# A two-block network on one core: six adds and subtractions per norm pair shared with GpSimd, RoPE copies issued by ScalarE, and the last top-k rounds moved ahead of the softmax

## The reference

```python
def rmsnorm(x, g):
    y = x32 * lax.rsqrt(jnp.mean(x32 * x32, axis=-1, keepdims=True) + EPS)
    return (y * g.astype(jnp.float32)).astype(x.dtype)

def second_block(x, ...):
    for l in range(DEPTH_2):
        h = rmsnorm(x, attn_norm[l])
        z = h @ w_in[l]            # q, k, v of branches A to D, index heads, gates
        yA = forgetting_attention(...)                       # softmax over 512 keys, causal
        yB = dsa_attention(rope(qB), rope(kB), vB, rope(qI), rope(kI), wI)
             # index scores, lax.top_k(score, 128), softmax over the selected keys
        r  = retention(rope(qC), rope(kC), vC)
        yD = sliding_window_gqa(rope(qD), rope(kD), vD, sinks)
        x = x + merged @ w_out[l]
        h = rmsnorm(x, ffn_norm[l])
        x = x + (silu(a) * b) @ w_down[l]
    return rmsnorm(x, final_norm)
```

## Time and profile before

| | us |
|---|---|
| median of 3 runs | 3597.19 |
| lowest and highest | 3596.74, 3599.80 |
| the profiled execution's own time | 3599.8 |
| its span from first to last instruction | 3598.5 |
| granted TensorE clock, mean | 0.989 |

### The profile page before, as it was taken

The page is one execution under the profiler, slowest core; times in us unless marked ns, Lnnn a source line. Parts: engine busy times, 40 slices in busy tenths (PEclk is TensorE's granted clock), DMA queues, the critical chain, the costliest instruction groups (busy, mean ns, idle before and its releaser), DMA issues.

```text
span 3598.5 us, 44824 instructions
## 1 busy us (share of the span) xinstructions
PE 3455.8 (96%) x17234; PEld 2744.8 (76%) x17234; DVE 1636.0 (45%) x3017; ACT 1437.1 (40%) x2442; POOL 1395.3 (39%) x627
## 2 busy tenths in 40 slices
PE   6999989988999999999999999999999999999998
PEld 4778889776678887877776778887876776778886
DVE  7986464647430014764453243143855453234143
ACT  3223354554532223354443344343354443334342
POOL 3454434321234443434332434444434333334443
PEclk9999999999999999999999999999999999999999
DMA  7664345321122323222222222323323222222322
GB/s 299 201 245 164 110 157 166 103 94 55 51 71 90 103 87 103 88 68 91 77 78 82 92 81 87 103 91 112 96 76 89 76 73 90 82 82 94 100 93 84
DMA packets 118420, 376.41 MB, mean 105 GB/s; under 512 B 15424, under 2 KB 16320, under 8 KB 117952
## 3 DMA queue, kind: packets, MB, share of 16 engines
q1 hardware_dynamic: 115728, 367.88, 31.6%
q10 hardware_dynamic: 2480, 5.68, 0.5%
HBM read 359.86 MB, written 2.10 MB: 101 GB/s over the span
## 4 chain that ended last, share of the span: by engine, by line
PE 80%; DVE 9%; ACT 4%; issue 3%; DMA 1%; POOL 1%; SPq 0%; ACTq 0%; DVEq 0%; POOLq 0%
PE ps L1389 24%; PE ps L1391 23%; PE ps L1390 23%; DVE b L2273 2%; PE ps L1649 2%; PE ps L1668 2%; ACT b L1731 1%; PE ps L1631 1%; POOL b L2636 1%; DVE b L2309 1%; PE ps L1432 1%; PE ps L1627 1%; PE ps L1691 1%; PE ps L1702 1%; DMA b<-in_w 1%
## 5 line engine op out<-in xcount | busy, mean ns | idle before, releaser
L2636 POOL TENSOR_TENSOR b<-b,b 128x1024 fp32r<-128x1024 f32 (+2 forms) x579 | 1325.1, 2289 | 2131.9 <-ACT b L1731 2129.0
L1389 PE MATMUL ps<-b,b 128*128 128x512 f32 (+1 forms) x4720 | 1793.3, 380 | 67.6 <-POOL b L2636 32.6
L1391 PE MATMUL ps<-b,b 128*128 128x512 f32 (+1 forms) x4720 | 1754.0, 372 | 0.0
L1390 PE MATMUL ps<-b,b 128*128 128x512 f32 (+1 forms) x4720 | 1753.8, 372 | 0.0
L1389 PEld LDWEIGHTS ps<-b,b 128*128 128x128 f32 x4720 | 890.6, 189 | 300.3 <-issue 99.3
L1391 PEld LDWEIGHTS ps<-b,b 128*128 128x128 f32 x4720 | 890.5, 189 | 160.8
L1390 PEld LDWEIGHTS ps<-b,b 128*128 128x128 f32 x4720 | 892.0, 189 | 155.3 <-issue 5.0
L1731 ACT ACTIVATE b<-b 128x1024 fp32r<-128x1024 f32 (+2 forms) x622 | 606.6, 977 | 266.5 <-PE ps L1391 235.6
L2185 DVE SCALAR_TENSOR_TENSOR b<-ps,b,b 128x511 f32<-128x511 f32 x88 | 66.0, 750 | 364.1 <-ACT b L1782 364.1
L2273 DVE CUSTOM_DVE_ANT_0 b<-b,b,b 128x1024 bf16<-128x1024 f32 x112 | 219.5, 1960 | 17.3 <-DMA b<-in_ada 5.8
L1792 ACT ACTIVATE b<-b 128x512 fp32r<-128x512 f32 (+1 forms) x110 | 64.9, 590 | 399.2 <-DVE b L2194 296.5
(11 more groups left out here) (235 smaller groups left out, 2406.1 us busy)
## 6 DMA issues: line engine op xcount, KB each, us to landing
b<-in_w SPq DMA_DIRECT2D x458, 512.0 KB, 3.5
b<-in_ada SPq DMA_DIRECT2D x88, 512.0 KB, 5.3
b<-in_w SPq DMA_DIRECT2D x80, 384.0 KB, 3.1
b<-in_w SPq DMA_DIRECT2D x80, 320.0 KB, 2.9
b<-b SPq DMA_DIRECT2D x176, 64.0 KB, 2.0
b<-in_const SPq DMA_DIRECT2D x24, 256.0 KB, 3.9
b<-in_x SPq DMA_DIRECT2D x1, 2048.0 KB, 16.7
out<-b SPq DMA_DIRECT2D x8, 256.0 KB, 2.0
```

The lines of the kernel that those rows point to most:

```text
L1389: pe.matmul(out, a[0], b[0], start=first, stop=False)
L1390: pe.matmul(out, a[0], b[1], start=False, stop=False)
L1391: return pe.matmul(out, a[1], b[0], start=False, stop=last)
L2636: then(pool.tensor_tensor(wlo[j % NS][:, 0:nk * w], raw[j % NR][:, 0:nk * w], whi[j % NS][:, 0:nk * w].bitcast(F32), ALU.subtract), "lop", j)
```

## The change

Three edits.

1. In all four addnorms the addition to the residual of tiles 1, 3 and 5 goes from DVE to POOL (new event `anp`). In prenorms 5 to 8 the low part of tiles 1, 3 and 5 goes from DVE to POOL (`pnp`). Each such POOL instruction waits for POOL's previous one (`behind`) and for its producer. The instructions are the same, 128x512 subtractions and additions (128x256 in addnorm 1). That is 12 additions and 12 subtractions.
2. The four RoPE DMAs of each tile are issued by ACT right behind its copy, after a wait for that copy, instead of by SP.
3. The last 11 steps of `select(3)` stay in the stage before, so that all 60 selection steps are woven there; `heads("A")` runs without them. The two 8-wide result vectors of MAX8 lie in the first columns of `stat`, which branch A writes too, and so the first maxima of A wait for the finished mask `("m8", l, 3)`.

```diff
-PN = {0: dict(norm=0, N=L), 1: dict(norm=1, N=LC), ...
-      5: dict(norm=9, N=L), 6: dict(norm=10, N=L), 7: dict(norm=11, N=L), 8: dict(norm=12, N=L)}
+PN = {0: dict(norm=0, N=L, low=False), 1: dict(norm=1, N=LC, low=False), ...
+      5: dict(norm=9, N=L, low=True),
+      6: dict(norm=10, N=L, low=True), 7: dict(norm=11, N=L, low=True), 8: dict(norm=12, N=L, low=True)}
...
-        B, last = select(1) + select(2) + select(3)[:9], select(3)[9:]
+        B = select(1) + select(2) + select(3)
         S += weave(F, [do("gap")] * 6 + [do("wi", l=l), do("fg1", l=l), do("gap")] + B[:8] + [do("fg2", l=l)] + B[8:], 1.0)
-        rounds = heads("A")
-        for k, step in enumerate(last):
-            rounds[k + 1].append(step)
...
-        S += weave(F, rounds, 0.325) + [do("takey", l=l, o=0, t=t) for t in range(4)]
+        S += weave(F, heads("A"), 0.325) + [do("takey", l=l, o=0, t=t) for t in range(4)]
...
+def low_of(p, i):
+    return "pnp" if PN[p]["low"] and i in (1, 3, 5) else "pnv"
...
+    def an_event(a, i):
+        return ("anp" if i in (1, 3, 5) else "anv", a, i)
...
 (SP)
-            elif k == "evac" and st["t"]["name"] in ROPES:
...
-                at.wait_ge(*n("ra", name, l, i))
-                for o in range(0, 128, 32):
-                    sp.dma_start(ropes[name][o:o + 32, i, :], Q[x % 2][o ^ 32:(o ^ 32) + 32, :]).then_inc(s[f"d_half{x % 2}"], 16)
 (ACT)
                     act.activation(Q[x % 2][:, :], b[:, :], ACT.Copy).then_inc(up("ra", name, l, i), 1)
+                    if name == "qb":
+                        at.wait_ge(*n("sqp", l, 3, 3))
+                    elif name in ("qd", "kc"):
+                        at.wait_ge(*n("s1", "A", l, 31))
+                    elif name == "qc":
+                        at.wait_ge(*n("s1", "B", l, 31))
+                    at.wait_ge(*n("ra", name, l, i))
+                    for o in range(0, 128, 32):
+                        act.dma_start(ropes[name][o:o + 32, i, :], Q[x % 2][o ^ 32:(o ^ 32) + 32, :]).then_inc(s[f"d_half{x % 2}"], 16)
 (DVE)
         def low(p, i):
+            if low_of(p, i) != "pnv":
+                return
...
-                at.wait_ge(*n("anq", a, i))
-                dve.tensor_tensor(dst[:, i, :], dst[:, i, :], q[:, 0:N], ALU.add).then_inc(up("anv", a, i), 1)
+                if i not in (1, 3, 5):
+                    at.wait_ge(*n("anq", a, i))
+                    dve.tensor_tensor(dst[:, i, :], dst[:, i, :], q[:, 0:N], ALU.add).then_inc(up("anv", a, i), 1)
...
-                        at.wait_ge(*n("sc", l, 3, 3))
+                        at.wait_ge(*n("m8", l, 3))
...
-                w, top = 128 * (j + 1), top2[:, x, :]
+                w, top = 128 * (j + 1), stat[:, 0:16, :].rearrange("p a b -> p (a b)")[:, 8 * x:8 * x + 8]
 (POOL)
+        def low(p, i):
+            if low_of(p, i) == "pnp":
+                slots = p_slots(p)
+                behind()
+                at.wait_ge(*n("pnh", p, i))
+                then(pool.tensor_tensor(HL[:, i, :], slots[i % len(slots)][:, :], HH[:, i, :].bitcast(F32), ALU.subtract),
+                     "pnp", p, i)
...
+            elif k == "pn":
+                if st["i"] > 0:
+                    low(st["p"], st["i"] - 1)
+            elif k == "pnlow":
+                low(st["p"], 7)
+            elif k == "an":
+                a, i = st["a"], st["i"]
+                if i in (1, 3, 5):
+                    slots, N, dst = a_slots(a), AN[a]["N"], CX if a == 1 else X
+                    behind()
+                    at.wait_ge(*n("anq", a, i))
+                    then(pool.tensor_tensor(dst[:, i, :], dst[:, i, :], slots[i % len(slots)][:, 0:N], ALU.add),
+                         "anp", a, i)
```

More of the change, by code:

```diff
@@ L189 @@
 NF = 5
-PN = {0: dict(norm=0, N=L), 1: dict(norm=1, N=LC), 2: dict(norm=3, N=L), 3: dict(norm=5, N=LC), 4: dict(norm=7, N=L),
-      5: dict(norm=9, N=L), 6: dict(norm=10, N=L), 7: dict(norm=11, N=L), 8: dict(norm=12, N=L)}
+PN = {0: dict(norm=0, N=L, low=False), 1: dict(norm=1, N=LC, low=False), 2: dict(norm=3, N=L, low=False),
+      3: dict(norm=5, N=LC, low=False), 4: dict(norm=7, N=L, low=False), 5: dict(norm=9, N=L, low=True),
+      6: dict(norm=10, N=L, low=True), 7: dict(norm=11, N=L, low=True), 8: dict(norm=12, N=L, low=True)}
 AN = {0: dict(norm=2, N=L), 1: dict(norm=4, N=LC), 2: dict(norm=6, N=L), 3: dict(norm=8, N=L)}
@@ L631 @@
     "dve_ret": ("c1v", "rd", "yc", "yg"), "dve_yl": ("nfl", "yl"), "dve_mg": ("mgl",), "dve_out": ("o",),
-    "pool_lo": ("lop",), "pool_rope": ("rp",),
+    "pool_lo": ("lop",), "pool_pre": ("pnp",), "pool_add": ("anp",), "pool_rope": ("rp",),
 }
 SEM_OF = {e: s for s, es in SIGNALS.items() for e in es}
+def low_of(p, i):
+    return "pnp" if PN[p]["low"] and i in (1, 3, 5) else "pnv"
 def number(S, stream):
@@ L665, in low @@
     def low(p, i):
-        mark("pnv", p, i)
+        mark(low_of(p, i), p, i)
     for s in S:
@@ L797, in number @@
             mark("anq", s["a"], s["i"])
-            mark("anv", s["a"], s["i"])
+            mark("anp" if s["i"] in (1, 3, 5) else "anv", s["a"], s["i"])
         elif k == "mixin":
@@ L1146, in program @@
     r = Region(RM)
-    stat, wi, top2 = r.get([128, 32, 5]), r.get([128, 4, 4]), r.get([128, 2, 8])
+    stat, wi = r.get([128, 32, 5]), r.get([128, 4, 4])
     PB = [ctx.enter_context(nc.psum_tensor(f"ps{i}", [128, 512], F32)) for i in range(8)]
@@ L1254, in n_ready @@
             return s["d_x" if nid == 0 else "d_cx"], 16
-        return n(*{2: ("y1", 0, i), 3: ("anv", 0, i), 4: ("y1", 1, i), 5: ("anv", 1, i), 6: ("wo", i),
-                   7: ("anv", 2, i), 8: ("y1", 2, i), 9: ("anv", 3, i), 10: ("xw", 0, i), 11: ("into", 3, i),
+        return n(*{2: ("y1", 0, i), 3: an_event(0, i), 4: ("y1", 1, i), 5: an_event(1, i), 6: ("wo", i),
+                   7: an_event(2, i), 8: ("y1", 2, i), 9: an_event(3, i), 10: ("xw", 0, i), 11: ("into", 3, i),
                    12: ("xw", 1, i), 13: ("into", 4, i)}[nid])
@@ L1370, in source @@
             if ver[0] == "pn":
-                at.wait_ge(*n("pnv", ver[1], k))
+                at.wait_ge(*n(low_of(ver[1], k), ver[1], k))
                 return (HC, LW) if ver[1] in (1, 3) else (HH, HL)
@@ L2305, in dve_program @@
                 if i >= len(slots):
-                    at.wait_ge(*n("pnv", p, i - len(slots)))
+                    at.wait_ge(*n(low_of(p, i - len(slots)), p, i - len(slots)))
                 elif p in (2, 3, 4, 5):
-                    at.wait_ge(*n("anv", p - 2, 7))
+                    at.wait_ge(*n("anp", p - 2, 5))
                 dve.scalar_tensor_tensor(slots[i % len(slots)][:, 0:N], n_tile(nid, i), gain_of(p)[:, i:i + 1],
@@ L2322, in dve_program @@
                 if i >= len(slots):
-                    at.wait_ge(*n(*("anv", a, i - len(slots))))
+                    at.wait_ge(*n(*an_event(a, i - len(slots))))
                 dve.scalar_tensor_tensor(q[:, 0:N], n_tile(nid, i), gn[:, an_gain[a], i:i + 1], Q[9][:, 0:N], ALU.mult,
                                          ALU.mult).then_inc(up("anq", a, i), 1)
-                at.wait_ge(*n("anq", a, i))
-                dve.tensor_tensor(dst[:, i, :], dst[:, i, :], q[:, 0:N], ALU.add).then_inc(up("anv", a, i), 1)
+                if i not in (1, 3, 5):
+                    at.wait_ge(*n("anq", a, i))
+                    dve.tensor_tensor(dst[:, i, :], dst[:, i, :], q[:, 0:N], ALU.add).then_inc(up("anv", a, i), 1)
             elif k == "mixin":
```

## The result

The changed kernel takes 3651.8 us (median of 4 runs, 3650.1 to 3655.7), the kernel before in the same comparison 3596.97. The ratio is 1.0153, its 95% interval 1.0136 to 1.0171: **slower by 54.8 us**. The forecast was 3606, its range ended at 3620. The side was right and the size was not.

What follows compares the result with a forecast made beforehand. PE was taken as the bound, so only what ends its waits matters. Norms 6.0 + 2.0 - 0.6, RoPE DMAs 1.5 and selection 0 made 8.9 us, giving 3606 from the median 3597.19; range 3593 to 3620.

Steps and rivals of the forecast that it cites:

- I take +1.5: RoPE tiles: issuing the four DMAs from ACT, 2.5 us of ACT per tile, adds 1.5 us in all.
- mostly taken up: RoPE stages: two to three rounds lie between a maximum and its transposes, so a 2.5 us ACT delay mostly disappears.
- The upper bound, +10: RoPE DMAs: at worst each of the four PE stalls behind an ACT copy grows by 2.5 us, +10.
- PE waits behind ACT in branches B and D of under 3 us in all: Branches B and D: sign by which the forecast would show, PE waiting for ACT less than 3 us in total.
- ACT becomes the limit of branches B and D: Rival for these branches: 24 tiles cost PE 0.5 to 1 us each, total 3617 to 3628; chance 0.13.
- ACT's 57 of 75 us: Branch B's stage: ACT's busy time with the DMA issues, 57 us of 75, below PE's 72.6; argument against ACT as limit.
- Caught up: Start of branch A: late first maxima are made up before their transposes three rounds later, so moving selection costs 0.
- up to 4.6: Start of branch A: the first maximum comes up to 4.6 us late after the moved selection, without a PE wait.
- +9 if the cover were gone: Selection, upper bound: if the lateness in branch A were not hidden, 2 layers x 4.6 us = +9.
- 7.4 forecast: Norms: 12 low parts +6.0, 6 standing additions +2.0, 6 woven additions -0.6, so +7.4 us.
- POOL works beside DVE: Rival for the norms: both engines run side by side, so the kernel gets faster, 3588 us (3587 to 3594); chance 0.12.
- absorbed: Rival: POOL's turns fall where DVE waits for ACT, RoPE issues are hidden; 3597 to 3602 us, chance 0.27.

Runs made afterwards that it cites:

- e5: Kernel before with only the RoPE DMAs moved to ACT, issued behind the next weight chunk's high part instead of ahead of it: 3604.89 us against 3599.45.
- e1_norms: Kernel before with only the norms' additions and low parts of tiles 1, 3 and 5 moved from DVE to POOL: 3606.86 us against 3601.55.
- e2: Kernel before with only the four RoPE DMAs of each tile issued by ACT right behind its copy: 3639.3 us against 3601.55.

## Why the prediction was wrong

**"I take +1.5" for the RoPE DMAs: the step that failed.** It measured +37.8. The sizes under it were right: the issues take 2.44 us on ACT (2.4 said), the landing is 2.0 as before, ACT stays far from PE's load. The queue behind the issues was named too: "the next high part, exponentials and transposed copies". The term was mis-sized because the path was wrong: all of it was weighed as a delay of ACT, "mostly taken up" by the distance of two to three rounds. The high part was not followed on: it is what POOL's weight part waits for, the cosine product stands behind that on POOL, and DVE waits for the cosine product in order. e5 shows that a delay of ACT of the same length behind the high part is indeed mostly taken up (+5.4 instead of +37.8). The upper bound, +10 from the four small stalls behind an ACT copy, was taken from stalls that exist, and could not show a wait that did not exist yet. The sign that the prediction named for itself, PE waits behind ACT in branches B and D of under 3 us in all, came out at 26 (2.3 before).

The rival "ACT becomes the limit of branches B and D" named this very chain ("DVE waits for POOL's cosine, which stands behind the late weight part"), had a chance of 0.13 and a price of 0.5 to 1 us a tile. It measured 29.7 / 24 = 1.24 with edit 2 alone, above that price, 28.1 / 24 = 1.17 in the changed kernel. What spoke against it, ACT's 57 of 75 us, was no argument: ACT is not the limit, its order is. In B and D a part of the price is the clock: the windows below 1.00 give away 8.5 us in the changed kernel and 3.4 before.

**The landing.** The Trainium skill (Trainium Kernel Development and Optimization, section "Key Constraints") was right in what it says of the engines behind the queues: the DMAs landed as before, 2.0 us. It says that several issuers save the sequencer's issue time; here that time (2.44 us) had to be paid on a queue in which something urgent stood behind.

**"Caught up" for the selection: failed, smaller.** 0 was forecast; alone it costs +3.4, and with edit 2 the A stages lose 11.5 instead of 4.9. The "up to 4.6" us of lateness held (2.9 with edit 3 alone); that the changed kernel shows 4.0 is in part edit 2, and so no confirmation of the sum. The claim that it is caught up before the transposes looked at who needs the maxima. Nobody was late for them. What counted is what stands behind the waiting exponential on ACT, the evacuation of a `gt` tile. The bound "+9 if the cover were gone" would have held the two stages' gaps but not the clock behind them.

**Norms: right.** 7.4 forecast, 5.3 measured (2.9 to 9.0). By the traces (addnorm 1, forecast at 0, can't be told from the falls of the clock around it): addnorm 0 -0.6 (forecast -0.6 for the woven ones), addnorms 2 and 3 +0.9 each (1.0), prenorm 5 +1.1 and prenorms 6 to 8 +1.3 each (1.5). POOL and DVE take turns, and neither "POOL works beside DVE" nor "absorbed" holds.

**What stays open.** The three edits alone sum to 46.5, the changed kernel has 54.8. By the traces 2 us are the meeting of edits 2 and 3 in branch A; by the medians edits 2 and 3 together (40.8) do not exceed their sum, and the changed kernel is 8.7 above them and edit 1. That lies within what the intervals allow (about 6 us for each of the two large times and 3 for edit 1), and the changed kernel's trace is 7.4 behind after the first block, where the clock gives away 32.4 us (before 23.9, its second trace 29.1, e1_norms 32.4); no run settles it.

## What to carry to other kernels

When an instruction is put ahead of others in a queue, don't ask how busy that engine is. Follow the next instruction behind it through every engine that it releases, down to the one that PE waits for, and compare its end with what it used to hide behind: here a weight part of 2.4 us was free inside the 4.5 us between a copy and the arrival of its halves, and cost 1.2 us a tile once it began when they landed. And when a result comes late "without anybody needing it yet", look at what is queued behind the engine that waits for it; a PSUM evacuation there turns the lateness into a stall of PE, and the stall can bring a fall of the clock that costs as much again. Issuing the same four DMAs behind one instruction instead of ahead of it (+5.4 for e5 against +37.8 for e2) was worth 32 us.

## What was not expected of the hardware

- The same gap of 2.07 us of PE at the same place in the two layers: the granted clock stayed at 1.00 behind the one and fell to 0.78 and 0.79 behind the other, 1.6 us more.
- A POOL copy with one operand (0.94 us) holds up a DVE product as a subtraction with two does; the product ends 0.55 after it in both cases.
- DVE's normalization with 128 columns, 0.29 us undisturbed, is held up beside a weight part as well (2.33 us in the kernel before, in the row that follows; timeline of DVE). Waits of this kind are part of the kernel before.

```profile
1647.05 2.33 DVE L2538 TENSOR_SCALAR b<-b,b 128x128 f32<-128x128 f32 x1
```
